# An encoder layer on one core: input loads first, the next sequence's norm two projections later, the second norm in halves

## What is computed

```python
def rmsnorm(x, g):
    return x * lax.rsqrt(jnp.mean(x * x, axis=-1, keepdims=True) + EPS) * g

def encoder_layer(x, ...):
    xn = rmsnorm(x, norm1_g)
    a, hy, gates = jnp.split(xn @ w_in, [512, 2048], axis=-1)
    gate_a, gate_b = jnp.split(gates, 2, axis=-1)
    ya = multiscale_pool(a, pool_w, pool_scale) @ w_pool_out
    yb = hyena_mixer(hy, conv_w, conv_b, <filter network>, hyena_bias) @ w_hyena_out
    h = x + (sigmoid(gate_a) * ya + sigmoid(gate_b) * yb) @ w_o
    return h + peer(rmsnorm(h, norm2_g), peer_wq, peer_keys, peer_u, peer_v)

y_prompt, y_sample = (rmsnorm(encoder_layer(x), normf_g) for x in (x_prompt, x_sample))
```

## Time and profile before

| | us |
|---|---|
| median of 3 runs | 3221.85 |
| lowest and highest | 3213.39, 3231.14 |
| the profiled execution: time, span of its trace | 3234.54, 3232.6 |
| PE busy in the span | 2891.0 |
| DVE, POOL, ACT busy | 1682.3, 1555.5, 557.7 |

### The profile page before, as it was taken

One profiled execution on the slowest core, in us unless ns is written; L12 is line 12 of the kernel. 1 busy time (PEld: TensorE's weight loads), 2 busy tenths in 40 slices (PEclk: granted clock), 3 DMA queues, 4 the chain that ended last, 5 costly groups with the idle time before them and its releaser, 6 DMA issues.

```text
span 3232.6 us, 29056 instructions
## 1 busy us (share of the span) xinstructions
PE 2891.0 (89%) x10143; PEld 1449.7 (45%) x10143; DVE 1682.3 (52%) x3842; ACT 557.7 (17%) x1190; POOL 1555.5 (48%) x1335
## 2 busy tenths in 40 slices
PE   5999989667789889956799999999999999999996
PEld 3656648433334445524244444444444444443331
DVE  4341124798998635897465654455654444441111
ACT  3211122100104555646000000000000000000000
POOL 2211213266675444546656665556665555553343
PEclk9999989888999999988899999999999999999998
DMA  3322254398899899998999999999999999998886
GB/s 133 120 100 74 85 197 146 116 363 287 308 355 364 310 365 361 376 339 340 402 378 381 396 365 386 390 382 399 372 378 394 373 379 382 372 393 289 284 296 230
DMA packets 338536, 998.63 MB, mean 309 GB/s; under 512 B 31095, under 2 KB 109687, under 8 KB 335832
## 3 DMA queue, kind: packets, MB, share of 16 engines
q0 software_dynamic: 184320, 671.17, 54.8%
q1 hardware_dynamic: 152344, 300.45, 26.1%
q10 hardware_dynamic: 1728, 25.17, 1.9%
HBM read 950.26 MB, written 46.40 MB: 308 GB/s over the span
## 4 chain that ended last, share of the span: by engine, by line
PE 60%; DMA 8%; DVE 7%; POOL 2%; issue 2%; ACT 1%; another core or an unknown queue 0%; SPq 0%; DVEq 0%; ACTq 0%; POOLq 0%
PE job_ps L1534 20%; PE wide_ps L1518 19%; PE v_ps L1555 9%; DMA v_rows<-in_peer_v,row_t 4%; PE job_ps L635 3%; PE wide_ps L635 2%; DVE u_row L1764 2%; POOL u_row L1444 2%; PE gate_ps L635 2%; DMA u_row<-in_peer_u,row_u 1%; PE wide_ps L1506 1%; DMA hand<-tmp_gates 1%; PE job_ps L613 1%; PE gate_ps L1506 1%; DVE prod L193 1%
## 5 line engine op out<-in xcount | busy, mean ns | idle before, releaser
L1454 POOL DMA_INDIRECT v_rows<-in_peer_v,row_t x640 | 693.7, 1084 | 785.7 <-PE v_ps L1555 617.2
L1444 POOL DMA_INDIRECT u_row<-in_peer_u,row_u x640 | 739.0, 1155 | 369.8 <-issue 178.3
L1764 DVE CUSTOM_DVE_ANT_0 u_row<-u_row,x_tile 128x1024 f32<-128x1024 f32 x640 | 771.0, 1218 | 115.3 <-DMA u_row<-in_peer_u,row_u 112.5
L1518 PE MATMUL wide_ps<-hand,arena 128*128 128x384 f32 x2048 | 688.0, 490 | 0.0
L1534 PE MATMUL job_ps<-arena 128*128 128x512 f32 x1536 | 687.1, 596 | 0.0
L1518 PEld LDWEIGHTS wide_ps<-hand,arena 128*128 128x128 f32 x2048 | 385.0, 190 | 322.0 <-issue 83.8
L1534 PEld LDWEIGHTS job_ps<-arena 128*128 128x128 f32 x1536 | 287.3, 190 | 368.9 <-issue 339.0
L1555 PE MATMUL v_ps<-v_rows,diag 128*32 128x512 f32 x2560 | 372.3, 621 | 66.1 <-DMA v_rows<-in_peer_v,row_t 65.3
L1802 DVE TENSOR_TENSOR arena<-arena,job_ps 128x512 f32<-128x512 f32 x192 | 131.6, 686 | 479.9 <-PE job_ps L1534 422.4
L899 POOL TENSOR_TENSOR exact<-arena,exact 128x1024 fp32r<-128x1024 f32 x48 | 118.0, 2463 | 451.6 <-ACT exact L647 451.6
L1656 ACT ACTIVATE hand<-wide_ps 128x384 f32<-128x384 f32 x128 | 62.9, 491 | 1494.8 <-PE wide_ps L1518 1196.6
(11 more groups left out here) (285 smaller groups left out, 2441.5 us busy)
## 6 DMA issues: line engine op xcount, KB each, us to landing
arena<-in_peer_ut SPq DMA_DIRECT2D x128, 512.0 KB
arena<-in_peer_v SPq DMA_DIRECT2D x128, 512.0 KB
hand<-tmp_gates SPq DMA_DIRECT2D x32, 768.0 KB
tmp_gates<-arena ACTq DMA_DIRECT2D x10, 2048.0 KB
arena<-in_w_in SPq DMA_DIRECT2D x32, 512.0 KB, 3.5
hand<-in_w_in SPq DMA_DIRECT2D x32, 512.0 KB
u_row<-in_peer_u,row_u POOLq DMA_INDIRECT x640
v_rows<-in_peer_v,row_t POOLq DMA_INDIRECT x640
```

What stands on the lines that cost most here:

```text
L1444: pool.indirect_dma_start(u_row[n % NU][:], None, dram["peer_u"], bass.IndirectOffsetOnAxis(row_u[g % 2][:, e:e + 1], 0)).then_inc(u_in[n ...
L1454: pool.indirect_dma_start(v_row[n % NV], None, dram["peer_v"], bass.IndirectOffsetOnAxis(row_t[g % 3][:, t:t + 1], 0)).then_inc(v_in[n % N ...
L1518: last = pe.matmul(wide[j % 2][:, 0:TD], uw[j % NW][:, k * P:(k + 1) * P], x_t[:, k], start=k == 0, stop=k == KD - 1)
L1764: dve.tensor_tensor_reduce(out=u_row[n % NU][:], in0=u_row[n % NU][:], in1=xb[g % 2][:], scale=1.0, scalar=0.0, op0=ALU.mult, op1=ALU.add, ...
```

## The change

Four edits. First, on SP the four tiles of x are issued first and the identity behind them, on a semaphore of its own; then come the filter tables, the gain, the four weights, and the other five small tables. PE waits for the identity alone ahead of its first transpose, ACT and DVE wait for the small tables at z0, and PE at mix 0. Second, of norm 2 the roots, the scales and the first two tiles are behind z3 (ACT takes the roots at the head of its z4), while the squares stay at z2, and the transposes `n` follow z4 to z7 instead of z2 to z5. Third, norm 1 of the first sequence is done in two halves, two tiles behind each pass of `r`, and its first two normalised tiles are written behind the first pass. Fourth, for that its gain is issued at `("r", 0)`. The second sequence's order is as it was.

```diff
+    def load_ident(self, sp, dram):
+        sp.dma_start(self.ident[:], dram["ident"]).then_inc(self.ident_in, 16)
...
-        for dst, name in ((self.ident, "ident"), (self.conv_w, "conv_w"), (self.conv_b, "conv_b"),
+        for dst, name in ((self.conv_w, "conv_w"), (self.conv_b, "conv_b"),
...
+    def halves(self, p):
+
+        if self.ready:
+            return range(LT) if p else ()
+        return range(2 * p, 2 * p + 2)
...
                 sp.dma_start(self.x[:, tt], d["x"][self.seq][:, tt]).then_inc(self.x_in[tt], 16)
+            self.small.load_ident(sp, d)
+            yield -1.0
...
-            if (kind, n) == ("r", KD):
+            if (kind, n) == ("r", KD if self.ready else 0):
...
-        pe.wait_ge(S.here, S.ALL)
+        pe.wait_ge(S.ident_in, 16)
         for kind, n in self.units:
             yield self.begin[kind, n]
+            if (kind, n) == ("mix", 0):
+                pe.wait_ge(S.here, S.ALL)
...
-        act.wait_ge(S.here, S.ALL)
         yield 0.0
...
+            if (kind, n) == ("z", 0):
+                act.wait_ge(S.here, S.ALL)
             if (kind, n) == ("z", 2) and not self.ready:
                 for tt in range(LT):
                     squares(2, tt)
+            if (kind, n) == ("z", 4) and not self.ready:
                 roots(2)
...
-            elif kind == "r" and n % KD == KD - 1 and n // KD == 1:
+            elif kind == "r" and n % KD == KD - 1 and self.halves(n // KD):
                 act.wait_ge(self.w_used, self.at_w[kind, n] + 1)
-                for tt in range(LT):
+                for tt in self.halves(n // KD):
                     squares(1, tt)
-                roots(1)
+                roots(1, self.halves(n // KD), n // KD + 1 if not self.ready else 1)
...
-        dve.wait_ge(S.here, S.ALL)
         yield 0.0
...
+                if (kind, n) == ("z", 0):
+                    dve.wait_ge(S.here, S.ALL)
...
-                if (kind, n) == ("z", 1) and not self.ready:
+                if (kind, n) == ("z", 3) and not self.ready:
                     scales(2)
                     normalise(2, 0)
                     normalise(2, 1)
...
-                if p:
+                if self.ready and p:
                     scales(1)
+                if not self.ready:
+                    scales(1, self.halves(p), p + 1)
+                if p == self.ready:
                     normalise(1, 0)
                     normalise(1, 1)
...
-        if not ready and 2 <= n < 2 + LT:
-            first += [("n", 2 * n - 4), ("n", 2 * n - 3)]
+        if not ready and 4 <= n < 4 + LT:
+            first += [("n", 2 * n - 8), ("n", 2 * n - 7)]
...
+            pre = p.sync(sp)
+            next(pre)
             flt.load_first(sp)
-            pre = p.sync(sp)
             next(pre)
```

More of the change, by code:

```diff
@@ L261, in __init__ @@
         self.pool_w = m.sb(f"{tag}_pool_w", [P, CT, P])
-        self.here = m.sem(f"{tag}_small_in")
+        self.here, self.ident_in = m.sem(f"{tag}_small_in"), m.sem(f"{tag}_ident_in")
+    def load_ident(self, sp, dram):
+        sp.dma_start(self.ident[:], dram["ident"]).then_inc(self.ident_in, 16)
     def load(self, sp, dram):
-        for dst, name in ((self.ident, "ident"), (self.conv_w, "conv_w"), (self.conv_b, "conv_b"),
+        for dst, name in ((self.conv_w, "conv_w"), (self.conv_b, "conv_b"),
                           (self.bias, "hyena_bias"), (self.pool_scale, "pool_scale"), (self.pool_w, "pool_w")):
             sp.dma_start(dst[:], dram[name]).then_inc(self.here, 16)
-    ALL = 6 * 16
+    ALL = 5 * 16
 class Handed:
@@ L658, in squares, with roots @@
             act.activation(self.sq_next if w == 2 else self.sq, src, ACT.Square, accum_out=self.ss[:, w * LT + tt:w * LT + tt + 1]).then_inc(self.squared[w], 1)
-        def roots(w):
-            act.wait_ge(self.ms[w], 1)
-            c = slice(w * LT, (w + 1) * LT)
+        def roots(w, tiles=range(LT), times=1):
+            act.wait_ge(self.ms[w], times)
+            c = slice(w * LT + tiles[0], w * LT + tiles[-1] + 1)
             act.activation(self.rstd[:, c], self.ss[:, c], ACT.Sqrt).then_inc(self.root[w], 1)
-        act.wait_ge(S.here, S.ALL)
         yield 0.0
@@ L757, in vector, with scales @@
         s = Steps(dve, self.vsteps)
-        def scales(w):
-            c = slice(w * LT, (w + 1) * LT)
-            dve.wait_ge(self.squared[w], LT)
+        def scales(w, tiles=range(LT), times=1):
+            c = slice(w * LT + tiles[0], w * LT + tiles[-1] + 1)
+            dve.wait_ge(self.squared[w], tiles[-1] + 1)
             dve.tensor_scalar(self.ss[:, c], self.ss[:, c], 1.0 / D, EPS, ALU.mult, ALU.add).then_inc(self.ms[w], 1)
-            dve.wait_ge(self.root[w], 1)
+            dve.wait_ge(self.root[w], times)
             dve.reciprocal(self.rstd[:, c], self.rstd[:, c]).then_inc(self.inv[w], 1)
-            dve.wait_ge(self.inv[w], 1)
+            dve.wait_ge(self.inv[w], times)
             dve.wait_ge(self.gain_in, 32 if w == 1 and not self.ready else 16)
```

## The result

| | before | changed |
|---|---|---|
| median of 12 runs, us | 3224.34 | 3207.55 |
| lowest and highest | 3213.39, 3231.14 | 3200.65, 3211.6 |
| ratio of the two, 95% interval | | 0.9947 [0.9938, 0.9957] |
| span of the profiled execution | 3232.6 | 3205.5 |
| of it, first block (to SP's first load of the second) | 609.91 | 592.50 |

The account below looks back on a forecast made before the run. The first block's waits on PE were taken as the bound, passed in full through a barrier. Head 10.0, norm 2 5.5 and second norm 5.9 sum to 21.4 us; 3213.1 profiled, 12.7 lower against the median, gives 3200, range 3186 to 3214.

Parts of the forecast that it names:

- The bound and the barrier: Between the two blocks: whatever the first block gains or loses arrives in full at the end, unless the second gives it back.
- The head: Start of the first block: with x issued first, the first tile is normalised at 17.3 instead of 27.36, 10.0 us earlier.
- the landing of the tables: At the head: filter tables, queued behind x and the identity, land at 10.3, so DVE's filter argument ends at 16.7.
- Norm 2 later: In the first block's projections: 10.3 us of idle time and slow clock removed, less new waits, 5.5 us won; bounds 8.3 and 1.1.
- The new wait: PE idles ahead of the tap pair behind z4, waiting for the first decay behind z3; 2.5 us taken, 2.0 to 4.1.
- the price of the clock: Slow matmuls on PE after the idle time behind z4: bounds 0 and 3.6 us, half taken, 1.8.
- the wait that stays: PE's idle 3.42 us at 110.67, ahead of the 16 transform matmuls, for two DVE passes behind z5; forecast unchanged.
- The wait for the filter column: PE behind a0 waits for a column queued on SP behind the last transposes and four tables; 0.5 us taken, 0 to 1.5.
- The second norm: End of r to first query projection: done in halves, only two tiles left at the end; 5.9 us won, 3.5 to 7.5.
- The new queues take back half: Rival over all three parts: head gains 6.3, norm 2 1.1, second norm 3.5; 10.9 us in all, 3211; chance 0.17.
- The head was not without effect: Rival at the head: issue order doesn't matter or something other than `pool_w` releases the squares; 11.4 us left, 3210; chance 0.04.
- SP's wait at z7: Rival: SP's wait for the last transposes delays weights, 42 us lost, 3242; held harmless up to some 20 us; chance 0.03.

Follow-up runs that it names:

- the filters-first kernel: The changed kernel with the five filter tables loaded ahead of x again, run twice; second block from 585.20 and 584.57, against 592.50 in the changed kernel.
- the second edit alone: The kernel before with only norm 2 of the other sequence moved two projections later; second block from 602.53 against 609.91, projections 152.6 us against 158.6.
- the two kernels that were run twice: The changed kernel, second block from 592.50 and 591.24, and that kernel with filter tables ahead of x, from 585.20 and 584.57, each rerun unaltered.

## Why the prediction was right, and where it was off

**The bound and the barrier.** Right. What the first block gained, 17.4 us, is what the ratio shows, 17.1. The forecast of 3200 is 7.5 us below the measured 3207.55. 2.5 of them are the kernel before, whose median was 3221.85 in the three runs at hand and 3224.34 in twelve. The gain is 4.0 short of the 21.4 in the traces: 1.4 at the head, 4.2 at norm 2 and 0.2 at the second norm are missing, and 1.8 came that nobody had forecast. The start of the second block in the trace of before was 609.91:

```profile
609.91 0.33 SPq L1345 DMA_DIRECT2D x_tile<-tmp_xn  x1
```

and in the changed kernel:

```profile
592.50 0.34 SPq L1365 DMA_DIRECT2D x_tile<-tmp_xn  x1
```

**The head**, 10.0 forecast, 8.6 measured. The chain was the right one: the filter tables through DVE's argument, with the sums waiting for nothing, and the small tables free. The first square came at 4.87, ahead of the 6 to 7 named, without effect. The term that was mis-sized is the landing of the tables, 10.3 forecast and 11.81 measured. The last x tile was in by 9.15, so its bytes came as reckoned; the identity and the five tables, last issued at 5.46, needed 2.7 us more, and not the 1.1 that their 0.41 MB take at 388 GB/s. The rate was what I had wrong, as two windows of the changed kernel show (the last numbers are the DMA share and the GB/s):

```profile
5.00:9.00 4.00, 0.00 (x0) 0.00 (x0) 0.00 (x0) 3.31 (x6) 0.00 (x0) 1.00 1.07 369
9.00:11.00 2.00, 0.00 (x0) 0.00 (x0) 0.00 (x0) 1.84 (x3) 0.00 (x0) 1.00 1.01 178
```

The DMA engines are as busy in the second window as in the first and move half as much. By the fit of the Trainium skill (page "DMA: Bandwidth & Descriptors", section "Anatomy of one DMA") the estimate was 8.5 and further off; the page gives the fit for a single DMA issued from GpSimd, and here ten stood in SP's queue. I also didn't ask whether x had to be ahead of the tables at all; the filters-first kernel shows 2.6 to 2.8 us left there.

**Norm 2 later**, 5.5 forecast. Measured 1.3 in the changed kernel and 6.0 alone. The new wait was named at its place and in its size: 2.5 forecast, 2.50, 2.45 and 2.41 measured. The step that failed is the price of the clock. I took half of the 3.6 us as a mean for "falls or doesn't fall" behind the new wait, and no change for the wait that stays. In the changed kernel it fell: the stretch behind the new wait took 11.5 us instead of 8.4, 3.1; and the 3.41 that I had carried over unchanged came with 1.8 us more of slow clock than before. The wait for the filter column, 0.5 taken and 1.5 at most, was 1.77 and 1.96; it is as named, behind SP's wait for the last transposes and the four tables. These three make 4.4 us, which is what the forecast has too much here, 4.2. (10.3 less 2.5, 3.1, 1.8 and 1.8 is 1.1.) The 6.0 of the edit alone are near the forecast by luck: there the clock cost nothing behind the new wait, where 1.8 was priced, and 1.1 less than before behind the one that stays, but the wait for the column took 2.2 and the slow clock behind it another 1.6, where 0.5 was priced. With these terms the sum is 5.2; the other 0.8 is not assigned.

**The second norm**, 5.9 forecast, 5.7 measured. The last square starts at 450.29, behind the adds, the table load is gone from its place, and the copies follow the split at 452.73. The idle time of 6.92 ahead of the last two tiles looks as bad as the 9.03 before, but stands behind the first two tiles' transposes and not ahead of them.

**The rivals.** "The new queues take back half" is nearest in time but not in kind: it had all three parts at their worst, and in fact two were near their forecast and one was at its bound. The head was not without effect. SP's wait at z7 was harmless for the weights, as held. A stall growing behind a0 was named among the things that would make me wrong, and it did grow, to 1.77, 1.3 us over what was taken and beyond the bound of 1.5.

**What agreed by chance.** 8.6, 1.3 and 5.7 are 15.6 of the 17.4. The other 1.8 belong to no edit: 0.6 lie behind the first query projection, and 1.2 are the `f` units, whose slow stretch behind an unchanged idle time of 4.8 was shorter in the changed kernel's trace (and in most of the other traces) than in that of before.

## What to carry to other kernels

When a stall goes, price the clock for every idle stretch that stays as well: at one and the same place in the program an idle time of 2.5 us cost 2.5 in some kernels and 5.6 in others, and that is a reason to remove it and not to shorten it. When loads are put in a new order, ask which is the last that the first computation needs over all engines, the small ones too, and put those with few bytes ahead; and after each reordering on one queue look for what was pushed back behind it. Where a part of the program that nothing touches scatters by as much as the change is worth (here by 13.7 us), measure the change by the time at which the trace enters that part.

## What was not expected of the hardware

The granted clock behind one and the same idle time (2.4 to 2.5 us, same work on both sides) was 0.50 in four traces and 1.00 in three, and twice the same in each of the two kernels that were run twice. The length of the idle time alone does not settle it. The unchanged 3.4 us ahead of the transforms did the same: the 16 matmuls behind it took 9.8 us in the changed kernel, 8.0 before, and 7.0 in the second edit alone. And so did the wait for the column: behind 1.77, 1.83 and 1.96 us the 16 matmuls took 6.5 us, behind 1.87, 1.93, 1.99 and 2.23 they took 8.2. In the three traces that kept the full clock behind the first two waits it fell behind this one.

Five filter tables, 0.35 MB, and the identity behind the 2.1 MB of x landed 2.7 us behind the last of x, although their bytes are 1.1 us at the 388 GB/s of the earlier trace rows. From 9 to 11 us the DMA share was 1.01 and the rate 178 GB/s, against 369 from 5 to 9. What made the rate fall was not tried; most of their bytes are in the table of 64x1024, whose lines are as long as those of x.
